# Retention pairs placed between gated-delta pairs, with the next gated-delta pair prepared inside them

## The reference

```python
h = rms_norm(x, norm_w)
proj = jnp.einsum('btd,de->bte', h, w_in)
...
# A: 4 heads of retention, chunks of 128
scores = jnp.einsum('bhncd,bhnsd->bhncs', q, k) * decay_mat[None, :, None]
...
y_ret = from_heads(rms_norm(o_ret, ret_norm_w[:, None, :])) * jax.nn.silu(rg)
# B: 6 heads of gated delta rule, chunks of 64, after a causal convolution of 4 taps
qkv = jax.nn.silu(causal_depthwise_conv(gqkv, conv_w))
...
y_gdn = from_heads(rms_norm(o_gdn, gdn_norm_w)) * jax.nn.silu(gz)
# C: 6 heads of attention, softmax over one block of 256 with ALiBi
y_moba = from_heads(o_moba) * jax.nn.silu(mz)
y = jnp.concatenate([y_ret, y_gdn, y_moba], axis=-1)
return x + jnp.einsum('btd,de->bte', y, w_out)   # the second projection
...
```

## Time and profile before

| | |
|---|---|
| median of 3 runs | 561.47 us (560.76 to 561.64) |
| the profiled execution, its own time | 561.29 us |
| its span, first to last instruction | 559.5 us |
| PE busy | 543.0 us, 97% of the span |
| DVE, ACT, POOL busy | 332.7, 282.7, 89.1 us |
| mean granted clock of TensorE | 0.997 of full speed |
| mean busy share of the DMA queues' packets (the weights) | 58.8% |

### The profile page before, as it was taken

The page is one execution under the profiler, slowest core; times in us unless marked ns, Lnnn a source line. Parts: engine busy times, 40 slices in busy tenths (PEclk is TensorE's granted clock), DMA queues, the critical chain, the costliest instruction groups (busy, mean ns, idle before and its releaser), DMA issues.

```text
span 559.5 us, 8847 instructions
## 1 busy us (share of the span) xinstructions
PE 543.0 (97%) x3456; PEld 465.6 (83%) x3456; DVE 332.7 (59%) x524; ACT 282.7 (51%) x457; POOL 89.1 (16%) x94
## 2 busy tenths in 40 slices
PE   3999999998999999999999999999999999999997
PEld 3887888887888878888888988888888888888885
DVE  2776886767678597446464356475456447655451
ACT  4766654445544653355654554564455546433340
POOL 1002122012230112111221121132131212000000
PEclk9999999998999999999999999999999999999999
DMA  9997654555345554546387648747765656487711
GB/s 276 205 294 169 186 151 122 144 131 134 76 114 152 150 134 118 153 125 174 90 213 203 175 122 229 185 116 189 188 163 151 180 185 189 159 273 222 230 56 37
DMA packets 149931, 91.81 MB, mean 164 GB/s; under 512 B 7843, under 2 KB 139138, under 8 KB 149762
## 3 DMA queue, kind: packets, MB, share of 16 engines
q1 hardware_dynamic: 148562, 88.95, 58.8%
q10 hardware_dynamic: 1328, 2.31, 1.2%
HBM read 89.13 MB, written 2.10 MB: 163 GB/s over the span
## 4 chain that ended last, share of the span: by engine, by line
PE 93%; ACT 3%; DMA 1%; DVE 1%; issue 0%; POOL 0%; ACTq 0%
PE pj L1132 37%; PE pj L1133 18%; PE pj L1154 5%; PE pj L1151 5%; PE pj L1153 5%; PE pj L1192 3%; PE pj L1129 2%; PE mx L1293 2%; PE mx L1303 2%; DMA cst<-table_dram 1%; PE pj L1197 1%; PE mx L1280 1%; PE pj L1128 1%; PE mx L1270 1%; PE mx L1182 1%; ACT w_hi L345 1%
## 5 line engine op out<-in xcount | busy, mean ns | idle before, releaser
L1132 PE MATMUL pj<-hT,w_hi 128*128 128x512 f32 x900 | 330.4, 406 | 0.0
L264 DVE TENSOR_TENSOR w_lo<-w_raw,w_hi 128x1024 fp32r<-128x1024 f32 x160 | 202.7, 1276 | 104.4 <-ACT w_hi L345 103.9
L1133 PE MATMUL pj<-hT,w_lo 128*128 128x256 f32 x900 | 252.3, 280 | 0.0
L345 ACT ACTIVATE w_hi<-w_raw 128x1024 fp32r<-128x1024 f32 x160 | 168.0, 1055 | 99.5 <-PE pj L1133 62.0
L1132 PEld LDWEIGHTS pj<-hT,w_hi 128*128 128x128 f32 x900 | 169.2, 188 | 37.3
L1133 PEld LDWEIGHTS pj<-hT,w_lo 128*128 128x128 f32 x900 | 170.1, 189 | 2.3
L658 POOL TENSOR_TENSOR raw<-ev 128x256 f32<-128x256 f32 x64 | 56.4, 882 | 322.0 <-ACT ev L353 321.9
L353 ACT ACTIVATE ev<-pj 128x512 f32<-128x512 f32 x64 | 37.9, 594 | 68.2 <-PE pj L1129 66.0
L1151 PE MATMUL pj<-w_hi,yT 128*128 128x512 f32 x128 | 50.3, 393 | 0.0
L1154 PE MATMUL pj<-w_lo,yT 128*128 128x512 f32 x128 | 49.9, 389 | 0.0
L1153 PE MATMUL pj<-w_hi,yT 128*128 128x512 f32 x128 | 49.8, 389 | 0.0
(11 more groups left out here) (206 smaller groups left out, 448.0 us busy)
## 6 DMA issues: line engine op xcount, KB each, us to landing
w_raw<-in_w_in_dram SPq DMA_DIRECT2D x256, 256.0 KB, 3.4
w_raw<-in_w_out_dram SPq DMA_DIRECT2D x64, 256.0 KB, 3.6
big<-in_x_dram SPq DMA_DIRECT2D x8, 256.0 KB, 5.3
out_dram<-sq ACTq DMA_DIRECT2D x8, 256.0 KB, 4.5
big<-in_x_dram SPq DMA_DIRECT2D x1, 1024.0 KB, 5.1
big<-in_x_dram SPq DMA_DIRECT2D x2, 512.0 KB, 7.7
cst<-table_dram SPq DMA_DIRECT2D x1, 682.0 KB, 4.6
cst<-table_dram ACTq DMA_DIRECT2D x1, 196.0 KB, 7.4
```

What stands on the lines that cost most here:

```text
L264: eng.tensor_tensor(w_lo[:, n % NSPLIT, :], w_raw[:, n % NRAW, :], w_hi[:, n % NSPLIT, :].bitcast(F32), ALU.subtract).then_inc(S("lo"), 1)
L345: act.activation(w_hi[:, n % NSPLIT, :], w_raw[:, n % NRAW, :], ACT.Copy).then_inc(S("hi_done"), 1)
L1132: pe.matmul(pj[s][:, :], high, hT[:, kc].rearrange("p a t -> p (a t)"), start=first, stop=False)
L1133: ins = pe.matmul(pj[s][:, 0:T], low, hT[:, kc, 0, :], start=False, stop=False)
```

## The change

The order of the pairs becomes gated-delta 0, retention 0, gated-delta 1, retention 1, gated-delta 2, and then the three attention pairs as before. The preparation of gated-delta pair j + 1 moves out of gated-delta pair j and stands in the second half of the retention pair between them. A gated-delta pair's output is now always turned at the next base less 8, ahead of retention as before or ahead of attention, and no longer 14 units into the next gated-delta pair. ACT's and POOL's split of that output follows. No operation of the mixing is added or dropped.

```diff
-PAIRS = [("gdn", 0), ("gdn", 1), ("gdn", 2), ("ret", 0), ("ret", 1), ("moba", 0), ("moba", 1), ("moba", 2)]
+PAIRS = [("gdn", 0), ("ret", 0), ("gdn", 1), ("ret", 1), ("gdn", 2), ("moba", 0), ("moba", 1), ("moba", 2)]
...
-U_RET = {"tail": -8, "gram": -6, "s1": 2, "qs": 10, "o": 10, "tr": 30}
-U_MOBA = {"nrm": -6, "bc": 8, "score": 14, "pt": 32, "o": 40}
+U_RET = {"tail": -8, "gram": -6, "s1": 2, "qs": 10, "o": 10, "tr": 30, "decay": 50}
+U_MOBA = {"tail": -8, "nrm": -6, "bc": 8, "score": 14, "pt": 32, "o": 40}
...
@@ ACT, mix_gdn
-                if more:
-                    square_first(j + 1)
-                    advance(base + 109)
-                    tanh_kq(j + 1, 1)
-                    square_second(j + 1)
@@ ACT, mix_ret
                 split_y(p, Y_BLOCK["ret"] + 2 * j)
 
+                advance(base + 48)
+                tanh_kq(j + 1, 0)
+                advance(U["decay"] + 5)
+                decay_exp(j + 1)
+                square_first(j + 1)
+                advance(base + 109)
+                tanh_kq(j + 1, 1)
+                square_second(j + 1)
@@ DVE, mix_ret
                 gated_pair(p, mx[0], [sm[:, 96 + 2 * j + h:97 + 2 * j + h] for h in range(2)])
 
+                conv(j + 1, 0, 0)
+                advance(base + 41)
+                conv(j + 1, 0, 1)
+                advance(base + 53)
+                decay_clip(j + 1)
+                silu_kq(j + 1, 0)
+                advance(base + 61)
+                conv(j + 1, 0, 2)
+                decay_mask(j + 1)
+                advance(base + 93)
+                conv(j + 1, 1, 0)
+                advance(base + 101)
+                conv(j + 1, 1, 1)
+                advance(base + 109)
+                silu_kq(j + 1, 1)
@@ DVE, mix_moba
                 advance(U["nrm"])
+                gated_last_gdn(p, mx[0])
@@ PE, mix_gdn
-                    if l == 1 and p:
-                        stream(U["tail"])
-                        out_transposes(p - 1, mx[2])
...
-                    if l == 4 and j + 1 < GDN // 2:
-                        pe.wait_ge(S("g_norm"), j + 1)
-                        decay_rows(j + 1)
@@ PE, mix_ret
-                after_gdn = PAIRS[p - 1][0] == "gdn"
-                if after_gdn:
-                    stream(U["tail"])
-                    out_transposes(p - 1, mx[3])
+                stream(U["tail"])
+                out_transposes(p - 1, mx[3])
...
                 out_transposes(p, mx[0])
+                stream(U["decay"])
+                pe.wait_ge(S("os_full"), p + 1)
+                decay_rows(j + 1)
@@ PE, mix_moba
+                if after_gdn:
+                    stream(U["tail"])
+                    out_transposes(p - 1, mx[0])
```

More of the change, by code:

```diff
@@ L86 @@
 U_GDN = {"gram": START, "ktr": 16, "vtok": 40, "t5": 64, "x6": 68, "y6": 72, "v0": 76, "s1": 81, "ks": 85, "v1": 90, "o": 95,
-         "tail": 14}
+         }
 for _l in range(1, LEVELS - 1):
@@ L381, in advance @@
                         g, s = finished(v - TAP_AFTER)
-                        if 0 < g < GDN and s < 3:
+                        if g and PAIRS[g // 2][0] == "gdn" and s < 3:
                             first_tap(g, s)
@@ L493, in mix_gdn @@
                 U = {k: base + v for k, v in U_GDN.items()}
-                more = j + 1 < GDN // 2
                 advance(U["ktr"] - 4)
@@ L519, in mix_gdn @@
                     act.activation(gt[a:a + HALF, :, a:a + HALF], gs[a:a + HALF, :, :], ACT.Copy).then_inc(S("gt_wide"), 1)
-                if more:
-                    decay_exp(j + 1)
                 advance(U["v0"] + 1)
@@ L580, in mix_moba @@
                     act.activation(sq[:, h].rearrange("p c k t -> p (c k t)"), mx[(3, 2)[h]][:, :], ACT.Square).then_inc(S("m_sq"), 1)
+                split_last_gdn(p)
                 act.wait_ge(S("m_vtok"), j + 1)
@@ L700, in mix_moba @@
                 power(64, 80, 8).then_inc(S("m_pow"), 1)
+                advance(base + 1)
+                split_last_gdn(p)
                 advance(base + 33)
@@ L852, in mean_square @@
                     dve.tensor_tensor(sm[:, 104:108], sm[:, 48:52], sm[:, 112:116], ALU.mult).then_inc(S("o_ms0"), 1)
-                    dve.wait_ge(S("o_ms0"), p + 1)
+                    dve.wait_ge(S("o_ms0"), PAIRS[p][1] + 1)
                     dve.tensor_scalar(sm[:, 52:56], sm[:, 104:108], EPS, None, ALU.add).then_inc(S("o_ms"), 1)
@@ L954, in mix_gdn @@
                         conv(j, 1, 2)
[L955 to L958, removed]
                     else:
@@ L981, in mix_gdn @@
                         elif l == 5:
-                            if more:
-                                decay_clip(j + 1)
-                                conv(j + 1, 0, 2)
                             advance(base + 53)
@@ L988, in mix_gdn @@
                         query_norm()
-                        if more:
-                            decay_mask(j + 1)
                         advance(base + 69)
@@ L1001, in mix_gdn @@
                                              vr[:, 2 * h + 1, :], ALU.mult, ALU.add).then_inc(S("vr1"), 1)
-                if more:
-                    conv(j + 1, 1, 0)
                 advance(base + 85)
@@ L1009, in mix_gdn @@
                 ins.then_inc(S("os_full"), 1)
-                if more:
-                    silu_kq(j + 1, 0)
                 advance(base + 93)
                 mean_square(p, True)
-                if more:
-                    conv(j + 1, 1, 1)
                 advance(base + 101)
-                if more:
-                    silu_kq(j + 1, 1)
                 advance(base + 109)
@@ L1091, in mix_moba @@
                 dve.wait_ge(S("zg"), p + 1)
+                dve.wait_ge(S("y_lo"), p)
                 dve.scalar_tensor_tensor(yf[:, :, :], mx[1][:, :].rearrange("p (h t) -> p h t", h=2), 0.5, zg[:, p % 2, :, :],
@@ L1160, in block_ready @@
             def block_ready(b):
-                order = {"ret": 3, "gdn": 0, "moba": 5}
-                kind = "ret" if b < 2 else "gdn" if b < 5 else "moba"
-                p = order[kind] + b - {"ret": 0, "gdn": 2, "moba": 5}[kind]
+                kind, first = ("ret", 0) if b < 2 else ("gdn", 2) if b < 5 else ("moba", 5)
+                p = PAIRS.index((kind, b - first))
                 pe.wait_ge(S("y_lo"), p + 1)
@@ L1263, in mix_gdn @@
                 stream(U["gram"])
+                if p:
+                    pe.wait_ge(S("yf_done"), p)
                 def sums(first, i):
@@ L1273, in mix_gdn @@
                 pe.wait_ge(S("sq"), 3 * j + 2)
-                if j == 0:
-                    pe.wait_ge(S("clip_done"), 4)
+                pe.wait_ge(S("clip_done"), 4 * j + 4)
                 sums(0, 0).then_inc(S("k_norm"), 1)
@@ L1378, in mix_ret @@
                 U = {k: base + v for k, v in U_RET.items()}
-                after_gdn = PAIRS[p - 1][0] == "gdn"
-                if after_gdn:
-                    stream(U["tail"])
-                    out_transposes(p - 1, mx[3])
+                stream(U["tail"])
+                out_transposes(p - 1, mx[3])
                 stream(U["gram"])
                 pe.wait_ge(S("evac"), 8 * p + 7)
-                if not after_gdn:
-                    pe.wait_ge(S("yf_done"), p)
                 for h in range(2):
@@ L1419, in mix_moba @@
                 pt = [kq[:, h].rearrange("p c k t -> p (c k t)") for h in range(2)]
+                after_gdn = PAIRS[p - 1][0] == "gdn"
+                if after_gdn:
+                    stream(U["tail"])
+                    out_transposes(p - 1, mx[0])
                 stream(U["nrm"])
                 pe.wait_ge(S("evac"), 8 * p + 7)
-                pe.wait_ge(S("yf_done"), p)
+                if not after_gdn:
+                    pe.wait_ge(S("yf_done"), p)
                 for h in range(2):
```

9 lines of the change are left out of this document (removed).

## The result

The changed kernel takes 558.66 us, the median of five runs (557.88 to 559.3). The ratio to the kernel before, over the same five rounds, is 0.9949 with a 95% interval of 0.9935 to 0.9964: faster by 0.5%, 2.8 us. The profiled execution took 558.0 us, its span 556.2 us.

What follows compares the result with a forecast made beforehand. PE, busy 97% of the span, bounds the kernel. 561.29 − 2.15 − 1.69 − 0.81 + 2.07 = 558.71 us for the profiled execution, 558.9 us as median of the runs, range 557.6 to 561.2.

Steps and rivals of the forecast that it cites:

- The two waits for squares and their cause: Openings of gated-delta 1 and 2: PE's waits of 2.15 and 0.81 us go; squares stood behind a late copy's chain.
- 0.8 us to spare at the openings: Gated-delta 1 and 2: first square ready at 196.9, PE comes at 197.7, so no wait.
- The clock, 1.69 us: Gram products after gated-delta 1's opening: 3.66 us at the fallen TensorE clock against 1.97; the difference is saved.
- The new wait, 2.07 us of idle time: Unit 248, turn of gated-delta 0's output: PE arrives before `on`; bounds 1.57 to 2.30 us, including 0.5 for POOL.
- Does the clock fall again?: Behind the wait at unit 248: left open, "stays" likelier; a fall costs 1.7 us, total 560.6; chance 0.25.
- Moved, at no cost, with its cover: Preparation moved into retention's second half: low halves stay 1.6 to 1.7 us ahead of PE; cost 0, bound 0.5 per pair.
- rival (c): Small extra waits at transposes after gated-delta 1 and 2 or for retention low halves: 0.3 to 1 us, 559.6; chance 0.14.
- The gate product ahead of attention, and the two other turns: Gate product, about 1.0 us, falls in DVE's idle time; turns after gated-delta 1 and 2 have 0.4 us to spare: 0.

Runs made afterwards that it cites:

- experiment 8: Kernel before, but in gated-delta 1 ACT copies the finished section out ahead of the output's four squares, not behind them: 561.12 us, ratio 0.9988.
- experiment 2: Kernel before, with 18 unread identity transposes on PE at gated-delta 1's opening, ahead of its wait for squares: 559.13 us, ratio 0.9965.
- experiment 3: Changed kernel, but in retention the third section's convolution is deferred to base + 77 and the decay mask to base + 85, both from base + 61: 557.73 us, ratio 0.9936.
- experiment 6: Changed kernel, but POOL makes the low half of a retention pair's output at base + 81, not base + 33: 558.18 us, ratio 0.9942.
- experiment 1: Changed kernel, but after gated-delta 0 the output is turned at unit 255, not 248, behind retention 0's Gram products: 556.12 us, ratio 0.9913.
- experiment 5: Changed kernel with both the output turned at unit 255 and retention's convolution and decay mask deferred: 555.09 us, ratio 0.9889.
- experiment 7: Changed kernel with LATE = 4, not 8, so gated-delta 0 stands 4 units earlier: 556.13 us, ratio 0.9903.
- experiment 9: Changed kernel with LATE = 4 and POOL's split of the retention output at base + 81: 555.28 us, ratio 0.9885.
- experiment 4: Changed kernel, but after gated-delta 0 the output is turned at unit 244, 4 units earlier: 560.68 us over ten runs, ratio 0.9994.

## Why the prediction was right, and where its sum was not

The forecast was 558.9 us in 557.6 to 561.2, with 0.71 for faster; measured were 558.66 us. Its steps one by one:

- **The two waits for squares and their cause.** Right. They are gone, and experiment 8 removed the second one by the cause named, without any of the change's parts. Why the squares were late at the first one was not tested by itself. I had 0.8 us to spare at the openings. In the profile of the changed kernel the pair of last squares (L485) starts at 179.44 and takes 0.75 us; PE's sums wait for the first of the two, through near 179.8, and start at 180.69, 0.9 us later.
- **The clock, 1.69 us.** Right for the profiled execution, by experiment 2 (1.67 us, from Gram products at full speed). It is no fixed price: ten of the 37 runs of the kernel before beside the experiments have a mean clock of 0.992 to 0.994 and not 0.997, and in the profile of experiment 8 the same opening cost 1.52 us more.
- **The new wait, 2.07 us of idle time.** Right in place and cause; the size was 1.81 us, between the bounds of 1.57 and 2.30. The hold-up by POOL was there, 0.26 us and not the 0.5 that I took: the second low half began at 128.87 and took 1.48 us and not 1.22. POOL's addition had begun at 127.97, inside the first low half, and ended at 129.27, only 0.40 us after the second one began. DVE and then POOL:

```profile
127.44 1.22 DVE L264 TENSOR_TENSOR w_lo<-w_raw,w_hi 128x1024 fp32r<-128x1024 f32 x1 [0.58 <-ACT w_hi L345]
128.87 1.48 DVE L264 TENSOR_TENSOR w_lo<-w_raw,w_hi 128x1024 fp32r<-128x1024 f32 x1 [0.21 <-ACT w_hi L345]
130.27 0.15 DVE L860 TENSOR_TENSOR sm<-sm 128x4 f32<-128x4 f32 x1
```

```profile
127.97 1.30 POOL L656 TENSOR_TENSOR raw<-ev 128x256 f32<-128x256 f32 x1
```

- **"Does the clock fall again?"** Held open at 0.25 for yes. It did not in the profiled execution. By the mean clock it did in one of the five runs (0.997, 559.3 us, the slowest), and the other four have 0.999 or 1.000. Experiments 3 and 6 keep this wait: 0.997 in none of five runs and in three of four. That is four of fourteen in all, near the 0.25 given, while the 17 runs of experiments 1, 5, 7 and 9, without the wait, all have 0.998 to 1.000.
- **"Moved, at no cost, with its cover".** This step was wrong in size. It costs 0.69 and 0.49 us, 1.18 us in all by experiments 3 and 6, where I took 0 and at most 0.5 a pair. The walk had 1.6 to 1.7 us to spare. It gave every DVE step its undisturbed duration, though the same text charged POOL's hold-up at unit 248. Three steps in retention 0 took 1.02, 0.48 and 0.55 us longer than that (2.24 for 1.22, 2.00 for 1.52, 1.23 for 0.68), 2.05 us in all: the spare time and 0.4 us more, which is the wait of 0.44 us. By experiment 3 the place of two of these steps mattered as much as the hold-up: with them moved the waits go, though the first hold-up stays (2.25 us at 154.03). So rival (c), given 0.14, came in beside the forecast; its other half, late turns after gated-delta 1 and 2, did not.
- **The gate product ahead of attention, and the two other turns.** Right: no wait stands there.

That the total came out so near rests on errors that offset each other. From the unit ahead of the sums to the second unit behind the Gram products PE took 7.42 and 4.41 us at the two openings before (129.45 to 136.87, 197.17 to 201.58) and takes 3.32 us now (180.34 to 183.66): 4.10 + 1.09 = 5.19 us are removed, not 4.65. The new wait costs 2.07 us, by chance the number that I had for its idle time alone. A weight load of PE that had waited 0.3 us for the first pair's state copy, which stood behind a tap of the next pair on ACT, no longer waits (0.29 us at unit 223). Against this stand the 1.18 us in retention. −5.19 − 0.29 + 2.07 + 1.18 = −2.23 us; the section ends, counted from the first, gain 2.65. The larger part of the remaining 0.4 us has no one place. Of the distances from one matmul of the stream to the next, 1655 stand in both profiles with nothing between. Apart from those at the two waits for a low half they are 0.3 us shorter in sum, none by more than 0.03 us; why is not shown.

What stays open is what decides in which runs the clock falls behind a given idle stretch.

## What to carry to other kernels

On a kernel bound by one engine's in-order stream, a change of order is worth the waits it removes less those it adds, each at somewhat more than its idle time, and the slow clock behind them; so find for each moved step its distance to the consumer in units of the stream and compare it with the lag of the nearest place that already has this chain; the pair with the odd offset (`LATE`) is the one to check. When a queue is walked, charge the hold-up between DVE and POOL everywhere and not only at the place under suspicion: it was larger than the whole slack. When a wait remains, look at which routine stream step stands between the operand and its last input; moving one low half behind `on` and one POOL step by 48 units, two edits of one line, gave 3.1 us by the section ends, where the whole change had given 2.65.

## What the runs showed of the hardware

- **Behind the same idle stretch the clock fell in some runs and not in others.** In the kernel before, 2.15 us idle and 0.92 us of one-column matmuls were followed by a fallen clock in each of the 37 runs beside the experiments (mean granted clock 0.992 to 0.997); with 18 transposes of 128 columns in the idle time (experiment 2) it was 0.999 or 1.000 in all five. With 128-column transposes at once behind it, 3.21 us idle (experiment 4) brought the mean under 0.998 in seven of ten runs, and 1.81 us (the changed kernel, experiments 3 and 6) in four of fourteen. These cases differ in the length of the idle time and in what followed it, so the runs do not say which of the two counts. The Trainium skill (TensorE: Matmul & The Clock Gate, Part 1) says that the gate's timing runs free of the kernel; the split within one kernel in experiment 4 agrees.
- **DVE and POOL hold each other up for whole instructions.** Low halves of 1.22 us took 1.48, 1.76 and 2.24 us when they began with 0.40, 0.68 and 1.16 us of a POOL addition left: 0.14 us less than that is added each time. In the other direction POOL's addition of 128x256, 0.75 us in the median, took 1.30 when it began at 165.06, inside a low half. The Trainium skill (SBUF — State Buffer, "SBUF: two separate sides") states this as an exclusive lock, and experiment 6 agrees: with POOL elsewhere the 2.24 us became 1.23.
- **A recorded wait of PE costs more than its idle time:** 2.07 us for 1.81 (experiment 1), and 0.69 us for 0.44 (experiments 3 and 6).
